# Unread identity products put into five places of TensorE's queue in a long-convolution stage

## What is computed

```python
def fftconv(u, k, bias):
    L = u.shape[1]
    U = jnp.fft.rfft(u, n=2 * L, axis=1)
    K = jnp.fft.rfft(k, axis=0)
    y = jnp.fft.irfft(U * K[None], n=2 * L, axis=1)[:, :L]
    return y + u * bias.astype(jnp.float32)
...
filt = hyena_filters(S, filt_w1[l], filt_b1[l], filt_w2[l], filt_b2[l], filt_w3[l], filt_freq[l])
z = v.astype(f32)
for n, gate in enumerate((x1, x2)):
    k = bidir_kernel(filt[:, n, 0], filt[:, n, 1])
    z = gate.astype(f32) * fftconv(z, k, filt_bias[l, n])
y_b = z.astype(dt) @ w_b_out[l]
```

## Time and profile before

| | |
|---|---|
| time, median of 3 runs | 4069.21 us (4068.99 to 4070.24) |
| the profiled execution: its own time | 4070.25 us |
| its span | 4068.6 us |
| mean granted clock of TensorE | 0.969 |
| PE busy over the span | 3798.7 us (93%) |
| DVE busy over the span | 2868.6 us (71%) |
| ACT busy over the span | 1820.9 us (45%) |

### The profile page before, as it was taken

How to read it: one execution, slowest core, us unless ns; L and a number is a source line. 1 busy time by engine, 2 the same in 40 slices (tenths; PEclk the granted TensorE clock), 3 DMA queues, 4 the chain that set the end, 5 groups by cost and what they waited for, 6 DMA issues and landing times. The chain is left out here.

```text
span 4068.6 us, 41958 instructions
## 1 busy us (share of the span) xinstructions
PE 3798.7 (93%) x16652; PEld 2871.6 (71%) x16652; DVE 2868.6 (71%) x2592; ACT 1820.9 (45%) x1686; POOL 309.8 (8%) x286
## 2 busy tenths in 40 slices
PE   8989987899999799999999997889499999999998
PEld 3557765788877677777787443577388888888886
DVE  3645554888887765555244698964698888888887
ACT  3234421777776224433011110210277777777776
POOL 0000000111110100000000000000000101011110
PEclk9999999899999999999999998999799999999999
DMA  3012025899997732223244333143499999999998
GB/s 115 6 54 76 17 90 186 322 398 398 399 399 293 246 112 66 67 68 101 81 133 152 124 114 104 52 148 122 179 364 378 373 381 368 382 369 381 374 378 314
DMA packets 422716, 883.12 MB, mean 217 GB/s; under 512 B 21994, under 2 KB 118609, under 8 KB 421428
## 3 DMA queue, kind: packets, MB, share of 16 engines
q1 hardware_dynamic: 381524, 754.45, 51.3%
q0 software_dynamic: 26896, 97.17, 6.8%
q10 hardware_dynamic: 14160, 29.63, 1.9%
HBM read 784.98 MB, written 96.21 MB: 217 GB/s over the span
## 5 line engine op out<-in xcount | busy, mean ns | idle before, releaser
L2281 DVE TENSOR_TENSOR moe_w_rest<-moe_w_w,moe_upper 128x2048 fp32r<-128x2048 f32 x384 | 862.6, 2288 | 163.1 <-ACT moe_upper L2184 87.0
L2184 ACT ACTIVATE moe_upper<-moe_w_w 128x2048 fp32r<-128x2048 f32 x192 | 357.3, 1909 | 243.5 <-PE moe_y_ps L2148 108.1
L2281 DVE TENSOR_TENSOR moe_w_rest<-moe_w_w,moe_upper_w 128x2048 fp32r<-128x2048 f32 x192 | 431.0, 2286 | 14.6 <-ACT moe_upper_w L2202 14.3
L2202 ACT ACTIVATE moe_upper_w<-moe_w_w 128x2048 fp32r<-128x2048 f32 x192 | 357.5, 1910 | 133.7 <-PE moe_up_ps L2122 77.0
L2192 ACT ACTIVATE moe_upper<-moe_w_w 128x2048 fp32r<-128x2048 f32 x192 | 357.2, 1917 | 0.0
L2122 PE MATMUL moe_up_ps<-moe_upper,moe_x_upper 128*128 128x512 f32 x768 | 311.2, 405 | 0.0
L2122 PE MATMUL moe_gate_ps<-moe_upper,moe_x_upper 128*128 128x512 f32 x768 | 305.8, 398 | 4.7 <-DVE moe_x_rest L2294 4.7
L2148 PE MATMUL moe_y_ps<-moe_upper_w,moe_hidT_upper 128*128 128x512 f32 x760 | 302.2, 398 | 3.6 <-DVE moe_hidT_rest L2299 3.0
L2122 PE MATMUL moe_gate_ps<-moe_w_rest,moe_x_upper 128*128 128x512 f32 x768 | 305.4, 398 | 0.0
L2122 PE MATMUL moe_gate_ps<-moe_upper,moe_x_rest 128*128 128x512 f32 x768 | 304.9, 397 | 0.0
L2122 PE MATMUL moe_up_ps<-moe_upper,moe_x_rest 128*128 128x512 f32 x768 | 304.0, 396 | 0.0
(11 more groups left out here) (592 smaller groups left out, 7663.6 us busy)
## 6 DMA issues: line engine op xcount, KB each, us to landing
moe_w_w<-in_expert_w_dram SPq DMA_DIRECT2D x96, 2048.0 KB, 16.6
moe_w_w<-in_w_gate_dram SPq DMA_DIRECT2D x64, 2048.0 KB, 10.5
moe_w_w<-in_w_up_dram SPq DMA_DIRECT2D x64, 2048.0 KB, 9.9
moe_w_w<-in_w_down_dram SPq DMA_DIRECT2D x64, 2048.0 KB, 9.5
tmp_y_rows<-moe_y ACTq DMA_DIRECT2D x32, 512.0 KB, 6.9
block_w_first<-in_w_in_dram SPq DMA_DIRECT2D x20, 512.0 KB, 3.7
tmp_h<-out_xn POOLq DMA_DIRECT2D x16, 512.0 KB, 3.2
tmp_spectra<-held_K ACTq DMA_DIRECT2D x8, 1024.0 KB, 5.0
```

The costliest lines, as they stand in the source:

```text
L2184: act.activation(half(upper1(c), h), half(weights.w1[c % 2], h), ACT.Copy).then_inc(m.w1_rounded, 1)
L2202: act.activation(half(upper2(i, c), h), half(weights.w2[c % 2], h), ACT.Copy).then_inc(m.w2_rounded, 1)
L2281: dve.tensor_tensor(half(rest, h), half(whole, h), half(upper, h).bitcast(F32), ALU.subtract).then_inc(done, 1)
```

## The change

A helper issues `n` products of the 128x128 identity with itself, in float32, into a part of a PSUM bank that nothing reads. It is called at five places on PE: ahead of the third filter product of pass 1 (32 products), at the start of I0 (36, behind a new wait on `product_ready`), at the start of I3 (32), ahead of bank 2 of I3 (10), and ahead of bank 4 of I3 (36). No other engine's instructions change.

```diff
+def stay_busy(nc, out, ident, n):
+
+    for _ in range(n):
+        nc.tensor.matmul(out, ident[:, :], ident[:, :], start=True, stop=True)
...
                     f = N_F * nth + 2 * t + d
+                    if f == 2:
+                        stay_busy(nc, inv_ps[0][:, 0:P], ident, 32)
                     if f >= 2:
 
                         pe.wait_ge(filt_ready, f - 1)
...
             H = [U_of(n, fh) for fh in range(HF)]
 
+            if n == 0:
+                pe.wait_ge(product_ready, HF)
+                stay_busy(nc, filt_ps[0][:, 0:P], ident, 36)
+            elif n == NP - 1:
+                stay_busy(nc, filt_ps[0][:, 0:P], ident, 32)
             pe.wait_ge(h_ready, HF * (n + 1))
             for bank in range(BANKS):
                 i, half = bank // 2, bank % 2
                 e = BANKS * n + bank
+                if n == NP - 1 and bank == 2:
+                    stay_busy(nc, filt_ps[0][:, 0:P], ident, 10)
                 if n == NP - 1 and bank == BANKS // 2:
+                    stay_busy(nc, filt_ps[0][:, 0:P], ident, 36)
 
                     pe.wait_ge(h_ready, HF * NP + 1)
```

More of the change, by code:

```diff
@@ L3896, in __enter__, with hyena_phase @@
         return m
-def hyena_phase(nc, block, m, tab, inputs, merge, v_x1, x2_T, z1):
+def hyena_phase(nc, block, m, tab, inputs, merge, v_x1, x2_T, z1, ident):
     NP = len(PASSES)
@@ L4522, in build_program @@
         ahead = AheadRows(nc, "w_o").open()
-        hyena_phase(nc, block, hy, tables2, inputs, merge, v_x1, x2_T, z1)
+        hyena_phase(nc, block, hy, tables2, inputs, merge, v_x1, x2_T, z1, ident)
         merge_phase(nc, block, merge, hy, a["w_b_out_2"], part_T, gate_T, merged_T, ahead, a["w_o_2"])
```

## The result

| | before | changed |
|---|---|---|
| median, and runs | 4068.11 us, 20 (4059.11 to 4072.93) | 4074.88 us, 20 (4068.55 to 4080.18) |
| ratio to before | | 1.0019, interval 1.0013 to 1.0025 |
| profiled execution: own time, span | 4070.25, 4068.6 us | 4072.7, 4071.1 us |
| mean granted clock | 0.969 | 0.973 |

The ratio is 7.7 us slower (5.3 to 10.2): real, but within the 0.2% that I called no change, though the interval reaches to 0.25%. The forecast was 4071.4 us, 3.5 us under the median. The clock rose, and the time rose with it.

What follows compares the result with a forecast made beforehand. DVE was taken to carry most of the convolutions and PE from I3 on. Terms -1.8 - 0.8 + 7.9 + 0 + 0 + 0 - 3.06 = +2.2 us gave a median of 4071.4 us, range 4067 to 4077.

Steps and rivals of the forecast that it cites:

- Price of an identity product: All five sets: 0.11 us a record, 0.22 us a product at 2.4 GHz, so 36 take 7.9 us.
- Rival (a): All sets: identity products don't hold the clock, later ones take 0.44 us each; +17 us, 4086 us; chance 0.08.
- First filters, -1.8: Ahead of the third filter product: 32 products fit the wait, filters start at full clock, K10 comes 1.8 us earlier.
- K10's first spectrum, -0.8: Behind PE's 2.26 us wait ahead of K10: untouched but timing-dependent; half taken between bounds 0 and 1.6 us saved.
- I0, +7.9: Start of I0: PE has no idle time and DVE waits for it, so 36 products cost all their 7.9 us.
- Rival (b): I0: its products are hidden because DVE sets the pace; sum -5.7 us, 4063.5 us; chance 0.04.
- I1, 0 within 0.7: Start of I1: clock down after 29.16 us of waiting in any case; 0, with 0.7 us either side.
- Start of I3, 0: Start of I3: 32 products fit the 7.39 us wait, but DVE takes bank 0 no earlier, so 0.
- Bank 2, 0 between -1.7 and +1.5: Ahead of bank 2 of I3: 10 products leave some 3.5 us idle; -1.7 if the clock holds, +1.5 if lost.
- Bank 4, -3.06: Ahead of bank 4 of I3: 36 products fit 8.77 us, and the bank takes 3.45 us, not 6.51.
- rival (c): I3: bank 6's narrow fit fails or 36 products overrun 8.77 us, losing bank 4's gain; +5.3, 4074.5 us; chance 0.13.
- theory 1: Follow-up runs: I0's products cost their own length on PE's path, other sets save as forecast; products covered by idle time cost nothing.

Runs made afterwards that it cites:

- only I3's front: Kernel before plus only the 32 products at the start of I3 and the 10 ahead of its bank 2: 4068.50 us, ratio 1.0000.
- only bank 4: Kernel before plus only the 36 products ahead of bank 4 of I3: 4068.99 us, ratio 1.0006.
- only filters: Kernel before plus only the 32 products among the first filters: 4069.43 us, ratio 1.0005.
- 36 products where nobody waits: Changed kernel with all five sets deleted, 36 products at the front of PE's 29 us wait ahead of I1: 4069.08 us, before 4066.44.
- without I0: Changed kernel without the 36 products and the wait on product_ready at the start of I0: 4063.45 us, before 4068.67.
- I1 instead: Changed kernel with I0's set moved to I1, as 56 products behind a wait on product_ready: 4063.95 us, before 4066.22.
- all waits: Changed kernel with I0's set moved to I1 (56 products), 9 added ahead of K10, 24 for 10 ahead of bank 2: 4059.86 us, before 4066.22.
- bank 2 with 24: Changed kernel without I0's set, with 24 products in place of 10 ahead of bank 2 of I3: 4063.68 us, ratio 0.9990.
- only I0: Kernel before plus only the 36 products with the wait on product_ready at the start of I0: 4077.30 us, ratio 1.0028.
- I0 doubled: Changed kernel with 72 products in place of 36 at the start of I0: 4080.26 us, ratio 1.0032.

## Why the prediction was right, and where it was off

*Price of an identity product, and that it holds the clock.* Right: 0.112 us a record, 8.04 us for 36 products where I took 7.9, the clock at 1.00 throughout. Rival (a) is out; it wanted records of twice the length inside I0's set. The row of transposes that I named for it told nothing: the clock rose there at about 256.4 (0.89 over 256 to 258), some 5.6 us after they began at 250.84, and behind bank 4's wait ordinary products stayed at the low pace for as long (from 2656.83 into the row of 2662.11). Whether transposes count is shown by no run here.

*First filters, -1.8.* Measured -1.81 (27.33 to 25.52), and -1.7 to -1.9 in every kernel that has the set.

*K10's first spectrum, -0.8, half of two bounds.* No execution shows the half. The wait of 2.26 us costs 1.7 us or nothing: with products among the filters it was cold in three profiles and warm in four; without them it was cold in all six. The mean over the seven is about -0.9, so the half was fair as an expectation, but in the profiled execution the term is 0. Why it was cold in six of six without the set and in three of seven with it stays open.

*I0, +7.9.* Measured +8.08 (128.13 to 136.21, with K10 cold in both), and +8.03 for the second set. Right in place and size. Rival (b) is out by DVE's wait of 10.33 us and by the doubled set.

*I1, 0 within 0.7.* +0.1 in the first profile, -0.7 in the second.

*Start of I3, 0.* Right: "only I3's front" leaves the stage as it was, though bank 0 is warm. DVE takes bank 0 late.

*Bank 2, 0 between -1.7 and +1.5.* The term measured +0.1 and -1.4. Ten products are too few for the wait: 3.19 us remain, and the bank was cold in four of the six profiles with ten, warm in one, in between in one (a first row of 1.71 us). With 24 products it was warm both times, and worth 1.4 us.

*Bank 4, -3.06.* Measured -2.95, in all eight profiles with the set; bank 6 fitted, and rival (c) is out, though its time, 4074.5 us, lies nearer to the measured 4074.88 than the forecast does. The nearness is chance: its mechanism is absent from every profile.

*Sum, +2.2.* In the first profile -1.81 + 8.08 + 0.09 + 0.11 - 2.95 = +3.52, of which 0.8 is the K10 term and the rest are tenths; in the second -0.49. The mean of the two stages is +1.6 against the mean of before. The steps held, within what the draws of the clock leave.

*From the sum to the time.* The time lay in the range and within 0.2%, but the point was off by 3.5 us, and the difference by more: a median of three, 4069.21, stood for the kernel before, and twenty runs of it gave 4068.11, with a mean of 4066.75. So I forecast +2.2, and the means differ by +7.8 (2.4) in the first pair of series and by +3.6 (2.4) in the second. That the profiled execution took 4072.7 us where I had written 4072.5 is luck: its stage was 3.5 us longer than before's and the rest of it 1.0 us shorter.

The timed differences are larger than those of the stage as well, +3.7 and -0.4. The same is seen elsewhere: the mean difference lies above the stage's by 3.8 (only bank 4), 4.1 (only filters), 3.1 (36 products where nobody waits), 2.2 (without I0), 4.0 (I1 instead), 2.4 (all waits), 3.3 (bank 2 with 24), 6.2 (only I0), 0.7 (I0 doubled), 0.6 (only I3's front). In twelve series the excess is always positive, 3.2 us on average. It could be a cost of a few microseconds for any of these edits that does not grow with the number of products (theory 3); the series of 36 idle products, only I0, only bank 4, only the filters and I1 instead lie nearer to it, and those without I0, of the changed kernel again and of I0 doubled nearer to theory 1.

The profiles don't show such a cost. Outside the stage the two executions of before take 3703.0 and 3701.3 us, and the twelve others 3700.1 to 3706.8, on average 3702.5, which is 0.4 more. And the twelve excesses are not twelve findings, since all are taken from the same two profiles of before. These two took 4069.2 us on average, 2.2 above the mean of before's series, 4067.0; the other twelve lay on average 0.5 below the mean of their own. With the 0.4 these make the 3.2 us, but for rounding. Of the 90 executions of before that the experiments were timed against, 25 took less than 4064.5 us, at a mean granted clock of 0.971; the other 65 had 0.969, and both profiles are of that slower kind. So the excess can be the draw of two executions, with no cost of the edits at all. Neither is shown, and only more profiles of the kernel before, of its fast executions too, could part them.

## What to carry to other kernels

Work that is added to hold TensorE's clock is free only in a wait of TensorE. Read the row ahead of which it is put: with no idle time in its brackets and an engine behind it that waits, each product costs its full length, and the mean clock of the page rises while the time does. Size each set to end just before the wait does, with the pace at the low clock for the part behind a long idle stretch, and fill short waits too or expect their cost by chance. A gain of 3 us that stands in the trace may be missing from the time, as for two sets here: time each set alone, and profile more than one execution of both kernels before you compare their traces.

## What the runs showed of the hardware

Behind a wait of 2.26 us the clock was low in nine of thirteen profiles and whole in four, with nothing between (43.03 to 43.13 us for the first spectra, or 41.44). Without products among the filters it was low in six of six, with them in three of seven, and those seven have alike rows around the wait. A wait of 3.14 to 3.19 us went either way too (first row of the bank 2.07, 1.71 or 1.13 us). So one trace of a kernel is one draw of several such steps: its stage here moved by 4.0 us between two profiles of the changed kernel, and by 0.3 between two of the kernel before. The Trainium skill ("TensorE: Matmul & The Clock Gate", Part 1, What's actually happening) says that how many products run at the low clock varies from run to run of the same kernel, since the monitoring is not tied to the kernel's start. The two profiles of the changed kernel agree, with 43.13 against 41.44 us for the first spectra; the two of the kernel before, with 43.10 and 43.03, don't show it.

Identity products that start behind 16.20 us of idleness run at 0.50 themselves, and the clock comes back within some 5 us of their start at 2449.74 (0.50 until 2454, 0.94 over 2454 to 2455, 1.00 behind that).
